# Values made with stationary weights and turned on TensorE, decay and beta spread from high and low parts

## The reference

```python
kv = (rmsnorm(c_kv, kv_norm) @ w_ukv).reshape(b, t, A_HEADS, 2 * A_HEAD_DIM)
k, v = kv[..., :A_HEAD_DIM], kv[..., A_HEAD_DIM:]
...
p = jax.nn.softmax(logits, axis=-1).astype(v.dtype)
return jnp.einsum('bqhk,bqkhd->bqhd', p, v_sel)
...
beta = jax.nn.sigmoid(beta_raw.astype(f32))
g = -jnp.exp(a_log.astype(f32)) * jax.nn.softplus(a_raw.astype(f32) + dt_bias.astype(f32))
...
gcum = jnp.cumsum(_to_chunks(g[..., None])[..., 0], axis=-1)
decay = jnp.exp(jnp.where(lower, gcum[..., :, None] - gcum[..., None, :], -jnp.inf))
kb = kc * bc[..., None]
```

## Time and profile before

| | us |
|---|---|
| median of 3 runs | 3022.74 (3021.61 to 3025.79) |
| the profiled execution's own time | 3021.39 |
| its span in the profile | 3019.6 |
| PE busy | 2989.1 (99%) |
| DVE busy | 1684.1 (56%) |
| ACT busy | 1363.3 (45%) |
| the chain that ended last, share on PE | 95% |

### The profile page before, as it was taken

One profiled execution on the slowest core, in us unless ns is written; L12 is line 12 of the kernel. 1 busy time (PEld: TensorE's weight loads), 2 busy tenths in 40 slices (PEclk: granted clock), 3 DMA queues, 4 the chain that ended last, 5 costly groups with the idle time before them and its releaser, 6 DMA issues.

```text
span 3019.6 us, 61906 instructions
## 1 busy us (share of the span) xinstructions
PE 2989.1 (99%) x24160; PEld 2937.0 (97%) x24160; DVE 1684.1 (56%) x2421; ACT 1363.3 (45%) x2006; POOL 169.8 (6%) x192
## 2 busy tenths in 40 slices
PE   9999999999999999999999999999999999999998
PEld 9889998999999999999999999999999999999998
DVE  4777675575554455545555555554456555455545
ACT  5555554553433343345544444444454443344443
POOL 0101010100000000000011011110000000000000
PEclk9999999999999999999999999999999999999999
DMA  5222222434445544454444444444545555555454
GB/s 205 98 92 81 108 80 98 165 146 172 176 165 172 183 176 168 171 169 164 158 167 167 155 164 153 167 154 166 194 153 181 181 185 181 191 186 188 181 178 156
DMA packets 77664, 482.58 MB, mean 160 GB/s; under 512 B 9093, under 2 KB 11525, under 8 KB 32784
## 3 DMA queue, kind: packets, MB, share of 16 engines
q1 hardware_dynamic: 77520, 481.26, 44.9%
q0 software_dynamic: 64, 0.21, 0.0%
HBM read 479.34 MB, written 2.10 MB: 159 GB/s over the span
## 4 chain that ended last, share of the span: by engine, by line
PE 95%; DVE 2%; ACT 1%; issue 1%; DMA 0%; DVEq 0%; SPq 0%; ACTq 0%
PE ps L475 94%; DVE w_lo L1801 1%; PE ps L1113 0%; PE ps L727 0%; DMA h<-in_x_t 0%; DVE u L1865 0%; ACT x_hi L1239 0%; ACT w_hi L1179 0%; DVE conv_acc L1944 0%; DMA raw<-in_w_mix_early 0%; DVE w_lo L1915 0%; ACT w_hi L1610 0%; PE ps L785 0%; ACT L1493 0%; DVE h L1871 0%
## 5 line engine op out<-in xcount | busy, mean ns | idle before, releaser
L475 PE MATMUL ps<-x_hi,w_hi 128*128 128x272 f32 (+1 forms) x4992 | 1447.3, 290 | 1.5 <-ACT x_hi L1239 0.8
L475 PE MATMUL ps<-x_lo,w_hi 128*128 128x272 f32 (+1 forms) x4992 | 1434.2, 287 | 0.5 <-DVE x_lo L1858 0.5
L475 PE MATMUL ps<-x_hi,w_lo 128*128 128x272 f32 (+1 forms) x4992 | 1425.9, 286 | 0.0
L1801 DVE TENSOR_TENSOR w_lo<-raw,w_hi 128x1024 fp32r<-128x1024 f32 (+2 forms) x952 | 1031.7, 1123 | 365.6 <-ACT w_hi L1179 353.6
L1179 ACT ACTIVATE w_hi<-raw 128x1024 fp32r<-128x1024 f32 (+1 forms) x902 | 849.4, 972 | 483.3 <-PE ps L475 394.3
L475 PEld LDWEIGHTS ps<-x_hi,w_hi 128*128 128x128 f32 x4992 | 942.1, 189 | 17.0 <-issue 12.8
L475 PEld LDWEIGHTS ps<-x_lo,w_hi 128*128 128x128 f32 x4992 | 939.8, 188 | 3.7 <-DVE x_lo L1858 1.5
L475 PEld LDWEIGHTS ps<-x_hi,w_lo 128*128 128x128 f32 x4992 | 941.9, 189 | 0.4
L475 PE MATMUL ps<-mid_hi,w_lo 128*128 128x256 f32 (+1 forms) x1920 | 543.1, 283 | 0.0
L475 PE MATMUL ps<-mid_hi,w_hi 128*128 128x256 f32 (+1 forms) x1920 | 542.8, 283 | 0.0
L475 PE MATMUL ps<-mid_lo,w_hi 128*128 128x256 f32 (+1 forms) x1920 | 542.4, 282 | 0.0
(11 more groups left out here) (294 smaller groups left out, 2205.2 us busy)
## 6 DMA issues: line engine op xcount, KB each, us to landing
raw<-in_w_up SPq DMA_DIRECT2D x176, 1024.0 KB, 4.8
raw<-in_w_ret_in SPq DMA_DIRECT2D x96, 1024.0 KB, 4.8
raw<-in_w_down SPq DMA_DIRECT2D x128, 704.0 KB, 4.0
raw<-in_w_heads SPq DMA_DIRECT2D x32, 1024.0 KB, 4.8
raw<-in_w_ret_out SPq DMA_DIRECT2D x32, 1024.0 KB, 4.8
raw<-in_w_mix_early SPq DMA_DIRECT2D x16, 768.0 KB, 4.4
raw<-in_w_latent SPq DMA_DIRECT2D x8, 1024.0 KB, 4.8
raw<-in_w_dsa SPq DMA_DIRECT2D x16, 256.0 KB, 2.5
```

The lines of the kernel that those rows point to most:

```text
L475: return nc.tensor.matmul(o, lhs, rhs, start=start, stop=stop)
L1801: V.tensor_tensor(w_lo[:, slot, cut], raw[:, slot, cut], w_hi[:, slot, cut], ALU.subtract).then_inc(lo_ready, count)
```

## The change

It has two parts, both in layer 0's mixer.

**Values.** They are now made as the keys are: six matmuls of 272 columns with the weights stationary, which leaves them with features on partitions. ScalarE copies them to `p_t` (`dsa_vt`), ahead of `gdn_ln` and not behind `gdn_rnorm`; `dsa_logits` waits for that copy. `dsa_turn` first turns the three blocks of `p_t` into BK_D1 (`dsa_vturn`), and ScalarE copies those to `v_h` (`dsa_values`, now two instructions) between `dsa_probs` and `dsa_turned`.

**Spread.** After the scans VectorE makes a high part of `gb8` (type fp32r, partitions 0 to 7 of `gb_two`) and a low part (partitions 32 to 39); the partitions between are zero. `gdn_select` works on 40 partitions and 548 values and writes fp32r; the two matmuls of `gdn_spread` have fp32r operands of 40 rows and 274 columns. `pick` and `ones_two` are made once, two copies of 8x8 and one of 40x128 on VectorE. `gb8` and `gsel` move into memory that other tiles use at other times. GpSimd's two clears of `ckv` give way to clears of `gb_two` and `pick`.

```diff
-            gb8 = sb("gb8", [HEADS, 2, LP], F32, first)
-            gsel = sb("gsel", [HEADS, 2, LP], F32, first)
+            gb_two = sb("gb_two", [32 + HEADS, 2, LP + 1], F32R, first)
+            gsel_two = sb("gsel_two", [32 + HEADS, 2, LP + 1], F32R, first)
+            ones_two = sb("ones_two", [32 + HEADS, P], F32R, first)
+            pick = sb("pick", [32 + HEADS, HEADS], F32, first)
...
-                for b in range(3):
-                    o = ps[:, BK_D0, b * P:(b + 1) * P]
-                    for k in range(2):
-                        xh, xl = ckv_hi[:, k, b * P:(b + 1) * P], ckv_lo[:, k, b * P:(b + 1) * P]
-                        wh, wl = w_hi[:, 1, (2 + k) * P:(3 + k) * P], w_lo[:, 1, (2 + k) * P:(3 + k) * P]
-                        mm(o, xh, wh, k == 0, False)
-                        mm(o, xl, wh, False, False)
-                        last = mm(o, xh, wl, False, k == 1)
-                last.then_inc(products, 1)
+                multiply(ps[:, BK_D0, 0:T], 1, 2, 2, lambda k: ckv_hi[:, k, 0:T], lambda k: ckv_lo[:, k, 0:T]
+                         ).then_inc(products, 1)
+
+            def dsa_vturn(i):
+                pe.wait_ge(DA.sem, DA.after("probs", i))
+                for b, (q0, n) in enumerate(BLK):
+                    last = nc.tensor.transpose(ps[0:n, BK_D1, b * P:(b + 1) * P], p_t[:, q0:q0 + n], ident[:])
+                last.then_inc(DP.sem, 1)
...
-                pe.wait_ge(DA.sem, DA.after("values", i))
+                pe.wait_ge(DA.sem, DA.after("vt", i))
...
             def dsa_turn(i):
-                pe.wait_ge(DA.sem, DA.after("probs", i))
+                dsa_vturn(i)
...
-                mm(ps[:, BK_2, 0:LP], ones[0:HEADS, :], gsel[:, 0, :], True, True)
-                mm(ps[:, BK_3, 0:LP], ones[0:HEADS, :], gsel[:, 1, :], True, True).then_inc(GP.sem, 1)
+                mm(ps[:, BK_2, 0:LP + 1], ones_two[:], gsel_two[:, 0, :], True, True)
+                mm(ps[:, BK_3, 0:LP + 1], ones_two[:], gsel_two[:, 1, :], True, True).then_inc(GP.sem, 1)
...
+            def dsa_vt(i):
+                act.wait_ge(products, dsa_at(i)[1] + 3)
+                nc.scalar.activation(p_t[:, 0:T], ps[:, BK_D0, 0:T], ACT.Copy).then_inc(DA.sem, 1)
+
             def dsa_values(i):
-                act.wait_ge(products, dsa_at(i)[1] + 3)
-                nc.scalar.activation(v_h[:].rearrange("p b t -> p (b t)"), ps[:, BK_D0, 0:3 * P], ACT.Copy
-                                     ).then_inc(DA.sem, 1)
+                act.wait_ge(DP.sem, DP.after("vturned", i))
+                nc.scalar.activation(v_h[:, 0:2].rearrange("p b t -> p (b t)"), ps[:, BK_D1, 0:2 * P], ACT.Copy)
+                nc.scalar.activation(v_h[0:16, 2], ps[0:16, BK_D1, 2 * P:3 * P], ACT.Copy).then_inc(DA.sem, 1)
...
                 if f is not None:
                     out_ln(f)
+                if d is not None:
+                    dsa_vt(d)
                 if g is not None:
                     gdn_ln(g)
                 if f is not None:
                     out_rnorm(f)
                 if g is not None:
                     gdn_rnorm(g)
-                if d is not None:
-                    dsa_values(d)
...
+            dve.wait_ge(LV.sem, LV.after("scan2"))
+            V.tensor_copy(gb_two[0:HEADS, :, 0:LP], gb8[:]).then_inc(LV.sem, 1)
+            dve.wait_ge(LV.sem, LV.after("two_hi"))
+            V.tensor_tensor(gb_two[32:32 + HEADS, :, 0:LP], gb8[:], gb_two[0:HEADS, :, 0:LP], ALU.subtract
+                            ).then_inc(LV.sem, 1)
...
             def gdn_select(i):
-                V.tensor_scalar(gsel[:], gb8[:], ident[0:HEADS, ds1(i)], None, ALU.mult).then_inc(GV.sem, 1)
+                V.tensor_scalar(gsel_two[:], gb_two[:], pick[:, ds1(i)], None, ALU.mult).then_inc(GV.sem, 1)
```

More of the change, by code:

```diff
@@ L194, in trunk @@
             cq_lo = sb("cq_lo", [P, 4, T], F32R, first)
-            ckv_hi = sb("ckv_hi", [P, 2, 3 * P], F32R, first)
-            ckv_lo = sb("ckv_lo", [P, 2, 3 * P], F32R, first)
+            ckv_hi = sb("ckv_hi", [P, 2, T], F32R, first)
+            ckv_lo = sb("ckv_lo", [P, 2, T], F32R, first)
             kidx = sb("kidx", [P, T], F32, first)
@@ L227, in trunk @@
             p_t = sb("p_t", [P, 432], F32, first)
+            gsel = dsa_s[0:HEADS, 0:2 * LP].rearrange("p (w t) -> p w t", w=2)
         with ExitStack() as second:
@@ L265, in trunk @@
         c3 = list(c2)
+        gb8 = carve(list(c2), [HEADS, 2, LP])
         q_h = carve(c3, [P, T])
@@ L311, in trunk @@
         LV = Steps(sem("lat_dve"), "pairs recip norm_q norm_kv lo shifted dt max abs one packed softplus nea decay "
-                   "scan0 scan1 scan2 widx cols01 cols3")
+                   "scan0 scan1 scan2 two_hi two_lo widx cols01 cols3")
         dots = sem("dots")
@@ L322, in trunk @@
         CA = Steps(sem("conv_act"), "silu0 silu1 silu2 gate")
-        DP = Steps(sem("dsa_pe"), "logits turned attended")
+        DP = Steps(sem("dsa_pe"), "logits vturned turned attended")
         DV = Steps(sem("dsa_dve"), "scored maxed recips y_lo")
-        DA = Steps(sem("dsa_act"), "values exped probs turned y_hi")
+        DA = Steps(sem("dsa_act"), "vt exped probs values turned y_hi")
         GP = Steps(sem("gdn_pe"), "sums spread scores turned tm0 "
@@ L1546, in mixer_body @@
                 if d is not None:
+                    dsa_values(d)
                     dsa_turned(d)
@@ L1617, in _ @@
             out_ln(g - 1)
+            dsa_vt(5)
             gdn_ln(g)
@@ L1620, in _ @@
             gdn_rnorm(g)
-            dsa_values(5)
             gdn_decayed(g)
@@ L1630, in _ @@
             gdn_tm0(g)
+            dsa_values(5)
             dsa_turned(5)
@@ L1640, in _ @@
             gdn_y(g, 4)
+            dsa_vt(6)
             split_last("mix4", EARLY_W, (1,))
-            dsa_values(6)
             gdn_y(g, 5)
@@ L1652, in _ @@
             split_last("mix7", EARLY_W, (1,))
+            dsa_values(6)
             dsa_turned(6)
@@ L1662, in _ @@
             split_last("mix8", EARLY_W)
-            dsa_values(7)
+            dsa_vt(7)
             split_last("mix9", EARLY_W)
@@ L1669, in _ @@
             split_last("mix11", EARLY_W)
+            dsa_values(7)
             dsa_turned(7)
@@ L1948, in _ @@
             dve.wait_ge(const_in, CONSTS0)
+            for r in (0, 32):
+                V.tensor_copy(pick[r:r + HEADS, :], ident[r:r + HEADS, r:r + HEADS])
+            V.tensor_copy(ones_two[:], ones[0:32 + HEADS, :])
             dve.wait_ge(drained, 8)
@@ L2014, in _ @@
             conv(0, 2, range(4))
-            dve.wait_ge(LV.sem, LV.after("scan2"))
+            dve.wait_ge(LV.sem, LV.after("two_lo"))
             def index_pair(i, slot):
@@ L2494, in _ @@
             G.memset(scratch[:], 1.0)
-            G.memset(ckv_hi[:, :, T:3 * P].bitcast(F32), 0.0)
-            G.memset(ckv_lo[:, :, T:3 * P].bitcast(F32), 0.0)
             G.memset(conv_in[:, :, 0:3], 0.0)
@@ L2501, in _ @@
             G.memset(conv_acc[:, 2, 0:P], 0.0)
+            G.memset(gb_two[:].bitcast(F32), 0.0)
+            G.memset(pick[:], 0.0)
             G.memset(p_t[0:64, P:T], NONCAUSAL)
```

## The result

| | before | after |
|---|---|---|
| median (lowest to highest) of 20 runs each, us | 3022.66 (3020.27 to 3027.20) | 3028.46 (3025.13 to 3034.95) |
| the profiled execution's own time | 3021.39 | 3027.84 |
| its span | 3019.6 | 3026.1 |

What follows compares the result with a forecast made beforehand. It took an ACT and DVE chain from the end of dsa_q to bound gdn_tm0 in loop rounds; 1.1 + 0.75 + 0 - 0.55 + 0.5 = +1.8 us on 3021.39, plus 1.35 to the median, gave 3024.5, range 3017.5 to 3030.

Steps and rivals of the forecast that it cites:

- the class with the highest chance: Whole kernel: time within 0.2% (6 us) of the kernel before, no change that can be told; chance 0.75.
- main case: Whole kernel: 3022.5 to 3027, from the bounds of transposes and round 1 and the spread of runs; chance 0.60.
- Round 1, +1.1: Round 1: two new DVE instructions delay the last convolution, ACT and PE's restart by 1.1 us, bounds 0.6 to 1.3.
- Loop rounds, 5 x (0.25 - 0.1): Five loop rounds: each pays 0.25 us for three transposes and gains 0.1 by an earlier gdn_ln; +0.75 in all.
- my list of signs: Timeline after: round 3's spread waits about 1 us, gdn_tm0 over 1; transposes within 0.25; round 1 1.1 us later.
- Spread, 0.26: Spread on PE: two fp32r matmuls take 0.13 us each, 0.26 instead of 1.11; 0.85 less in 8 rounds.
- Round 2, 0: Round 2: the spread's saved 0.85 us go into the wait for the indexer's ReLU; no gain.
- g = 7, -0.55: Behind the loop, g = 7 with d = 5: gdn_tm0 starts some 0.8 us earlier, transposes cost 0.25; -0.55.
- d = 6 and 7, +0.5: Behind the loop: the values' saved 1.18 us are lost in waits twice, transposes cost 2 x 0.25; +0.5.
- Sum: Whole kernel: 1.1 + 0.75 + 0 - 0.55 + 0.5 = +1.8 us.
- The rival on the clock: Round 2 and around L785: longer waits bring clock falls, 3.0 us each; one 3027.5 (0.16), two 3030.5 (0.11).
- The rival that saved work counts: Eight rounds: all saved PE work is had, 14.2 us, giving 3009.6, or half, 3016; chance 0.13.

Runs made afterwards that it cites:

- waits_filled: The changed kernel with throwaway float32 matmuls in TensorE's waits of round 1, round 2, d = 6 and d = 7; 3024.07 us, ratio 1.0005.
- values_only: The changed kernel with the old spread put back (8 rows, float32, no high and low part); 3033.11 us, ratio 1.0034.
- spread_only: The kernel before with the new spread, third value block's stationary 16 columns wide, not 128, and v_h copied in two instructions; 3024.40 us, ratio 1.0006.
- before_fixes: The kernel before with the logarithm's table load ahead of the split and throwaway matmuls in round 1, round 2 and d = 7; 3022.04 us, ratio 0.9992.

## Why the prediction was right, and where not

The time lies in the range and in the class with the highest chance, within 0.2%. It lies outside the main case, 3022.5 to 3027: against the likeliest value of 3024.5 it is 4 us too slow, and that is one rival which came in beside the forecast. That 5.8 us is still under the line of 6 us is luck, not foresight. By its own words the forecast's single case was wrong: "It is wrong if [...] the clock falls a second time."

- **Round 1, +1.1.** Measured +1.33, and 1.39 back when the two instructions stand behind the convolution. The mechanism is right, the size over my upper bound of 1.3 by a hair.
- **Loop rounds, 5 x (0.25 - 0.1).** Measured 5 x 0.145. The two parts were each short by 0.08 (transposes 0.33, `gdn_ln` 0.18 earlier) and cancelled. The waits came where they were put: 1.08 at the spread (forecast 1.0), 0.80 at `gdn_tm0` (0.9, though my list of signs asked for over 1). My evidence for a wait at `gdn_tm0` in every round before, 4.3 us in 7 waits, was misread: on PE's matmuls the loop rounds show none.
- **Spread, 0.26.** Measured 0.45: the two matmuls start 0.23 us apart, as each of the four float32 records before did, not 0.13 as the products of the earlier trace rows. It is hidden by the wait ahead of it or behind it, so the sum doesn't feel it.
- **Round 2, 0.** Right in the queueing: the wait went from 1.21 to 2.05 (forecast 2.06). The sum priced nothing behind it, and the clock fell there.
- **g = 7, -0.55.** The shift went from 2.65 to 2.28, -0.37 with one head's transposes (0.33) in it: `gdn_tm0` came 0.70 earlier against the round before, forecast 0.8. Its idle time stayed at 1.41, where I had put a wait of 2.6 and a fall.
- **d = 6 and 7, +0.5.** The saved 1.18 us were lost in waits, which grew from 0.83 to 1.75 and from 1.24 to 2.43, as argued. Both waits brought a fall.
- **Sum.** Without the new falls the shift behind the mixer is 6.06 - 3.7 = 2.4 us (2.3 by waits_filled), forecast +1.8. The difference is some 0.3 us in rounds 1 and 2, 0.1 at g = 7 and 8 x 0.08 for the transposes, less 5 x 0.08 that `gdn_ln` gained over the forecast.
- **The rival on the clock.** Its mechanism was right: saved work turned into waits, and waits into falls. The step that failed is its price and its chance. I took 3.0 us for one fall, from round 1's 6.9 us; the new ones last half as long and cost 1.4 to 1.5. I gave 0.27 to any fall at all, and three came, the first behind the very wait that I had computed as 2.06. The two errors work against each other: three falls for 3.7 us, since a wait takes up 0.6 of them, against 6.0 for the two in the rival. Of round 1's own fall the price was near: 3.0 forecast, 2.7 measured in waits_filled.
- **The rival that saved work counts.** I held against it that the chain of `gdn_tm0` "starts ahead of the saving". That is wrong for the values. The 0.34 us of idle at `gdn_ln`, released by PE, said that the sums, and the values ahead of them, were on the path. I used the row for its 0.34 and did not follow what it meant. In the change as made it matters little, since ScalarE's table load and the new copy come last once the sums are 1.18 us earlier; with the load moved, the saving is had.

What stays open: why one loop round of values_only kept its clock and the other four did not, and why the same wait brings a fall in one profile and none in another; the slower pace in the last dense network; and the worth of round 1's 1.39 us in the median.

## What to carry to other kernels

Where a wait has two inputs that come 0.3 us apart, a saving on one is worth those 0.3 us until the other is moved too; try the two together, since each alone shows nothing (a loop round of 49.33 with the table load moved, 49.48 with the new values, 48.63 with both). On TensorE, work saved ahead of a wait is not free to save: price each wait that grows with a fall of the clock times its chance, and if it can't be closed, fill it. In the profiles here the waits of 1.75 to 2.07 us in round 2 and d = 6 had a fall with them in 9 of 13 cases, those of 2.43 in d = 7 in 7 of 7. When a forecast computes such waits itself, their falls belong into the sum and not into a rival.

## What the runs showed of the hardware

- The spread's two fp32r matmuls of 40 rows and 274 columns take 0.45 us, the two of float32 on 8 rows 1.11. The trace has two records for the former and four for the latter, and both kinds start some 0.23 us apart: fewer passes, none of them faster, and not the 0.13 us apiece of a stream of products.
- fp32r matmuls of 128 moving columns start every 0.11 us with 128 stationary columns and every 0.06 with 16 (spread_only). With 128, the stationary side sets the pace and not the moving one. The Trainium skill, TensorE: Matmul & The Clock Gate, section LDWEIGHTS (loading the stationary operand), counts a load by its columns, 128 / 1.2 = 107 ns; this trace agrees with 0.108 us. For 16 columns an estimate by that section is 13 ns; the trace has 60, so something else sets the pace there.
- In the mixer every fall of the clock lasted 3.4 us or 6.8, in all profiles. A short one cost 1.3 to 1.5 us on a path bound by TensorE, 1.15 to 1.2 in a loop round with slack ahead of `gdn_tm0`; a long one that began in a wait cost 2.7. A fall need not stand at a long wait: before_fixes, its wait in round 2 filled, has one at 171.7 us, and one at 506.3 behind a wait of 1.17 us.
- A logarithm on one column costs ScalarE 0.2 us and moves a 1.28 us table load to where the engine is idle in part (0.89 us); the split behind it starts 0.6 us later. The Trainium skill, ScalarE: Activation LUTs, section Table sets: the hidden batching unit, has logarithm and exponential in one set; here each has its own load in every round (L1500 and L1505, 1.28 us each). No run here tried to use one.
